# A two-sequence encoder layer with a 16-expert MoE: the last expert's rows added by matrix products instead of a scatter, and the last normalisation moved ahead of the overflow branch

## The chip, the cores and the metric

The kernel runs on one core of one Trainium2 chip. The metric is the device time of one execution in microseconds (us). Engines by the profile's names: PE (TensorE, the matrix unit) with PEld (its weight loads), DVE (VectorE), ACT (ScalarE), POOL (GpSimd) and SP (SyncE, which here only issues DMAs). Each engine runs its own list of instructions in order; they meet only through semaphores.

## The reference, cut to what matters

Two sequences of 256 tokens (T = 512 rows of D = 1024 floats, four tiles of 128 rows) pass a token mixer and then a grouped top-2 mixture of experts:

```python
x = layer_norm(ALPHA * x + token_mixer(x), ln1_g, ln1_b)
# grouped_moe: gates has two nonzero entries in each row of 16
for e in range(16):
    h = silu(xt @ w_e1[e]) * (xt @ w_e3[e])      # 1024 -> 512
    y = y + gates[:, e:e + 1] * (h @ w_e2[e])    # 512 -> 1024
out = layer_norm(ALPHA * x + y, ln2_g, ln2_b)
```

## The kernel before, in words

Weights come as 512 KB units (`load`, L530, on SP's queue) into rings of slots. ACT casts a unit to its float32r high part (`cast_hi`, L680), DVE forms the low part (`cast_lo`, L969), and PE makes three products for each (`three`, L1687 to L1689). In the token mixer the raw ring has six slots and the split ring three, so that the cast of unit u waits until PE has finished unit u - 3. Units 0 to 27 are the input projection; units 0 to 7 and 16 to 27 take 128 columns of the weight (pieces of 512 bytes in DRAM), units 8 to 15 take 512 columns (pieces of 2 KB). In SP's list, after unit 14 and before unit 17, only loads stand; at unit 17 SP stores the value rows (`v_scratch`, L563, 4 x 256 KB), waits for them, and at units 18 and 19 reads them back as windows (`v_win`, L571, 8 x 256 KB, an access pattern whose outer dimension is 4). ACT's list after the cast of unit 19 goes on with `keys(0)` (L711), then the cast of unit 20; PE's list has `scores(0)` (L1723), which needs `keys(0)`, between units 18 and 19.

In the MoE each expert has 128 slots. For each expert a one-hot tile `onehot` (token x slot) gives, by a product on PE, the token, row and gate of each slot; POOL gathers the tokens' rows (`gather`), PE computes the expert (`hidden`, `turn_h`, `output`: the 128 x 1024 result in PSUM banks 2 and 3), ACT scales it by the gates into `y` (`scale_y`, L892) and POOL scatters it (`scatter`, L1621) to `y_dram`, 2T rows: each token has a row in the lower half for its first expert and one in the upper half for its second. `lower_stored` says that experts 0 to 14 are stored; expert 15, the highest, is always a token's second expert, so it never writes the lower half. SP then loads `y_first` (L628, four tiles of 512 KB). After expert 15's scatter `all_stored` rises and SP loads `y_second` (L650).

Should any expert have more than 128 tokens, an `If` on the register loaded from `overflow` (each engine has one) runs further passes over all experts; with these inputs it is not taken and the engines jump to `Else`. In the kernel before this branch stands, on every engine, after expert 15 and ahead of the last sum.

The tail, from L1527 on DVE: for the four tiles x = ALPHA x + y_first (L1529); then for each tile x + y_second (L1535), its statistics (`bn_stats` twice L1538, `bn_aggr` L1540, `var_eps` L1542); POOL takes the root (`root`, L1570 and L1573). Tiles 0 and 1 are scaled on ACT (L954), multiplied by `ln2_g` on POOL (L1668) and get `ln2_b` on DVE (L1548); tiles 2 and 3 are centred and multiplied by `ln2_g` (L1545), then scaled with `ln2_b` (L1552) on DVE. SP stores tile t once it is ready, in the order 0 to 3 (L654), and waits for the stores.

```python
        sp.wait_ge(all_stored, 1)
        for t in range(TT):
            sp.dma_start(y_second[:, t, :], y_dram[T + t * P:T + (t + 1) * P, :]).then_inc(second_loaded[t], 16)
        for t in range(TT):
            sp.wait_ge(out_ready, t + 1)
            ...
        sp.wait_ge(out_stored, 16 * TT)
```

Of the kernel before, what the change touches and what calls it, by code (L numbers as in the profile page):

```python
# [17 lines left out]
P = 128  # L18
# [138 lines left out]
def encoder_layer(nc, A, out_prompt, out_sample):  # L157
# [18 lines left out]

    raw = sb(ctx, "raw", [RAW, UNIT])
# [45 lines left out]
    conv_odd = sb(early, "conv_odd", [W])  # L223
    early.close()
# [40 lines left out]
    y_second = sb(tail, "y_second", [TT, D])  # L265
# [35 lines left out]
    w_lo_more = sb(moe, "w_lo_more", [M_SPLIT - SPLIT, UNIT], F32R)  # L301
    xg = sb(moe, "xg", [2, D])
# [5 lines left out]
    hT_lo = sb(moe, "hT_lo", [4, SLOTS], F32R)  # L308
    y = sb(moe, "y", [2, D])
# [22 lines left out]
    halo_zero = sem("halo_zero")  # L332
    var_ready = sem("var_ready")
# [178 lines left out]
    def _(sp):  # L512
        def load(j, source, n, per=0, i=None):
# [5 lines left out]
            elif j >= U_MOE + RING:  # L519
                sp.wait_ge(lo_cast, nth(j - RING + 1, per, i))  # L520
            elif j == U_MOE:
                sp.wait_ge(unit_used, U_WO)
            elif j == U_MOE + 2 * MORE:
                sp.wait_ge(unit_used, U_WO + 4)
            elif j == U_MOE + 3 * MORE:

                for t in range(TT):
                    sp.wait_ge(x1_ready[t], 1)
                    sp.dma_start(x1_dram[tokens_of(t), :], x1[:, t, :]).then_inc(x1_stored, 16)
# [21 lines left out]
        for u in range(U_MERGE):  # L551
# [5 lines left out]
            if 6 <= u < 14:  # L557
                for qr in range(ROWS):
                    load_bias((u - 6) % 2, (u - 6) // 2, qr)
            if u == 17:  # L560
# [65 lines left out]
        def load_first():  # L626
            for t in range(TT):
                sp.dma_start(y_first[:, t, :], y_dram[tokens_of(t), :]).then_inc(first_loaded[t], 16)  # L628


        sp.wait_ge(flag_ready, 1)
        with sp.register("over_sp") as reg:
            sp.reg_load(reg, overflow[0:1, 0:1])
            with sp.If(sp.snap(reg) > 0):
                with sp.Fori(0, EXPERTS) as e:
# [6 lines left out]
                load_first()  # L642
            with sp.Else():

                sp.wait_ge(lower_stored, 1)
                load_first()

        sp.wait_ge(all_stored, 1)
        for t in range(TT):
            sp.dma_start(y_second[:, t, :], y_dram[T + t * P:T + (t + 1) * P, :]).then_inc(second_loaded[t], 16)  # L650
        for t in range(TT):
            sp.wait_ge(out_ready, t + 1)
            o = (out_prompt, out_sample)[t // 2][0]
            sp.dma_start(o[tokens_of(t % 2), :], x1[:, t, :]).then_inc(out_stored, 16)  # L654
        sp.wait_ge(out_stored, 16 * TT)
# [3 lines left out]
    def _(act):  # L659
# [259 lines left out]
        for k in range(8):  # L919
# [4 lines left out]
            if k == 5:  # L924
                scale_y(j + 5, 15, 1, 0)
            if k == 7:
                scale_y(j + 7, 15, 1, 1)

        act.wait_ge(flag_ready, 1)
        with act.register("over_act") as reg:  # L930
            act.reg_load(reg, overflow[0:1, 0:1])
            with act.If(act.snap(reg) > 0):
                with act.Fori(0, EXPERTS) as e:
# [13 lines left out]
                act.nop()  # L947
            with act.Else():
                act.nop()


        for t in range(TT - 2):
            act.wait_ge(rstd_ready, 10 + t)
            act.activation(x1[:, t, :], x1[:, t, :], ACT.Identity, scale=rstd[:, t:t + 1],  # L954
                           bias=mu_rstd[:, t:t + 1]).then_inc(normalised, 1)
# [3 lines left out]
    def _(dve):  # L959
# [540 lines left out]

        with dve.register("over_dve") as reg:
            dve.reg_load(reg, overflow[0:1, 0:1])
            with dve.If(dve.snap(reg) > 0):
                with dve.Fori(0, EXPERTS) as e:
# [15 lines left out]
                dve.nop()  # L1520
            with dve.Else():
                dve.nop()

        for t in range(TT):  # L1527
            dve.wait_ge(first_loaded[t], 16)
            dve.scalar_tensor_tensor(out=x1[:, t, :], in0=x1[:, t, :], scalar=ALPHA, in1=y_first[:, t, :],  # L1529
                                     op0=ALU.mult, op1=ALU.add).then_inc(final_step, 1)  # L1530
        for t in range(TT):
            row = x1[:, t, :]
            dve.wait_ge(second_loaded[t], 16)
            dve.wait_ge(final_step, max(t + 1, 3 * t + TT))
            dve.tensor_tensor(row, row, y_second[:, t, :], ALU.add).then_inc(y_summed, 1)  # L1535
            dve.wait_ge(y_summed, t + 1)
            for k in range(2):
                dve.bn_stats(stats[:, t, k, :], row[:, k * 512:(k + 1) * 512]).then_inc(final_step, 1)  # L1538
            dve.wait_ge(final_step, TT + 3 * t + 2)
            dve.bn_aggr(mv[:, t, :], stats[:, t, :, :].rearrange("p k s -> p (k s)")).then_inc(final_step, 1)  # L1540
            dve.wait_ge(final_step, TT + 3 * t + 3)
            dve.tensor_scalar(var_eps[:, t:t + 1], mv[:, t, 1:2], EPS, None, ALU.add).then_inc(var_ready, 1)  # L1542
            if t >= 2:
                dve.wait_ge(ln2_loaded, 32)
                dve.scalar_tensor_tensor(out=row, in0=row, scalar=mv[:, t, 0:1], in1=ln2_g[:], op0=ALU.subtract,  # L1545
                                         op1=ALU.mult).then_inc(last_centred, 1)
                dve.wait_ge(scaled, TT + t - 1)
                dve.tensor_tensor(x1[:, t - 2, :], x1[:, t - 2, :], ln2_b[:], ALU.add).then_inc(out_ready, 1)  # L1548
        for t in (TT - 2, TT - 1):
            dve.wait_ge(last_centred, t - TT + 3)  # L1550
            dve.wait_ge(rstd_ready, 10 + t)
# [527 lines left out]
```

## Time and profile before

| | us |
|---|---|
| median of 3 runs (lowest, highest) | 815.1 (814.48, 816.12) |
| the profiled execution: its own time | 817.13 |
| its span on the core, first to last instruction | 815.3 |
| PE busy / DVE / ACT / POOL | 755.7 / 629.7 / 423.8 / 78.6 |
| mean granted clock of PE | 0.958 |

The rows further down come from this one execution; its own time is 1.8 us above its span. The clock is given as a share of 2.4 GHz. Times of rows are us from the span's start. A row of a timeline has start, duration, engine, line, operation, output<-inputs with shapes, the count of merged instructions, and in brackets the idle time before it with what ended it.

### The profile page before, as it was taken

Reading aid. Unit: us, or ns where it says so; the run is one execution under the profiler, and the core shown is the slowest. Engines: PE = TensorE matmul, PEld = TensorE weight load, DVE = VectorE, ACT = ScalarE, POOL = GpSimd, SP = SyncE. Lnnn points to the kernel's source line nnn. Section 1 sums busy time; section 2 is a strip of 40 time slices with the busy share of each in tenths; the row PEclk is TensorE's granted clock in tenths of the full one; section 3 lists DMA queues with packets and bytes.
Section 4 is the critical chain, followed back from the end, with each engine's and each line's share of the span. In section 5 each row is a group of like instructions: output and inputs, shape, how many; then the busy total and the mean of one; then the engine's idle time right before and its main releaser. Section 6 shows DMA issues by size and latency. Waiting matters only on the chain.

```text
span 815.3 us, 10978 instructions
## 1 busy us (share of the span) xinstructions
PE 755.7 (93%) x3559; PEld 621.5 (76%) x3559; DVE 629.7 (77%) x907; ACT 423.8 (52%) x568; POOL 78.6 (10%) x87
## 2 busy tenths in 40 slices
PE   4999999999999999999999859999999999999840
PEld 3888778888888888888888848888888888888630
DVE  5699977766678648344478659999999999999848
ACT  5421235456422246223222418888888888888701
POOL 5000000000000000000110310111111111111006
PEclk9999999999999999999999659999999999999965
DMA  9735556212223332323597548999999999996242
GB/s 300 234 94 145 150 148 164 78 53 77 78 78 104 103 100 79 107 81 101 184 374 246 214 154 279 375 361 368 372 379 377 383 379 373 364 378 236 87 174 104
DMA packets 129167, 171.96 MB, mean 211 GB/s; under 512 B 15386, under 2 KB 67334, under 8 KB 129110
## 3 DMA queue, kind: packets, MB, share of 16 engines
q1 hardware_dynamic: 121440, 154.95, 56.2%
q0 software_dynamic: 6752, 15.80, 5.4%
q10 hardware_dynamic: 934, 0.69, 0.3%
q8 instruction: 23, 0.38, 0.2%
q14 instruction: 18, 0.15, 0.0%
HBM read 164.06 MB, written 15.97 MB: 221 GB/s over the span
## 4 chain that ended last, share of the span: by engine, by line
PE 86%; DVE 7%; ACT 2%; DMA 2%; issue 1%; POOL 1%; DVEq 0%; SPq 0%; POOLq 0%; ACTq 0%
PE bank L1687 26%; PE bank L1689 26%; PE bank L1688 26%; PE bank L1951 2%; PE bank L1723 1%; DMA x_in<-in_x_sample_dram 1%; PE bank L1966 1%; PE bank L1906 1%; PE bank L1733 1%; PE bank L1941 1%; DVE stats L1538 1%; PE bank L1682 1%; ACT w_hi L680 1%; DVE w_lo L969 1%; DVE stats L1271 1%
## 5 line engine op out<-in xcount | busy, mean ns | idle before, releaser
L969 DVE TENSOR_TENSOR w_lo<-raw,w_hi 128x1024 fp32r<-128x1024 f32 x103 | 125.2, 1222 | 80.4 <-ACT w_hi L680 80.1
L680 ACT CAST w_hi<-raw 128x1024 fp32r<-128x1024 f32 x103 | 107.1, 1049 | 105.9 <-PE bank L1689 100.8
L1687 PE MATMUL bank<-xT_hi,w_hi 128*128 128x512 f32 x352 | 140.3, 399 | 2.8 <-DVE xT_lo L1007 1.8
L1689 PE MATMUL bank<-xT_hi,w_lo 128*128 128x512 f32 x352 | 138.7, 394 | 0.0
L1688 PE MATMUL bank<-xT_lo,w_hi 128*128 128x512 f32 x352 | 137.8, 392 | 0.0
L1687 PE MATMUL bank<-w_hi,xgT_hi 128*128 128x512 f32 x192 | 79.4, 413 | 1.6 <-DVE xgT_lo L1434 1.6
L1687 PEld LDWEIGHTS bank<-xT_hi,w_hi 128*128 128x128 f32 x352 | 66.6, 189 | 18.1 <-issue 3.6
L1689 PEld LDWEIGHTS bank<-xT_hi,w_lo 128*128 128x128 f32 x352 | 66.4, 189 | 15.2
L1688 PEld LDWEIGHTS bank<-xT_lo,w_hi 128*128 128x128 f32 x352 | 66.5, 189 | 14.1
L1689 PE MATMUL bank<-w_hi,xgT_lo 128*128 128x512 f32 x192 | 76.2, 397 | 0.0
L1688 PE MATMUL bank<-w_lo,xgT_hi 128*128 128x512 f32 x192 | 75.5, 393 | 0.0
L791 ACT ACTIVATE gate<-bank,vec 128x512 f32<-128x512 f32 x24 | 16.5, 689 | 84.6 <-PE bank L1689 84.5
L969 DVE TENSOR_TENSOR w_lo<-raw_more,w_hi 128x1024 fp32r<-128x1024 f32 x40 | 48.3, 1221 | 8.5 <-ACT w_hi L680 7.8
L969 DVE TENSOR_TENSOR w_lo<-raw_late,w_hi 128x1024 fp32r<-128x1024 f32 x40 | 48.2, 1221 | 3.4 <-ACT w_hi L680 2.7
L680 ACT CAST w_hi<-raw_more 128x1024 fp32r<-128x1024 f32 x40 | 41.2, 1047 | 7.5 <-PE bank L1689 7.5
L1039 DVE SCALAR_TENSOR_TENSOR conv<-conv_in,conv_col,conv 128x512 f32<-128x512 f32 x60 | 44.7, 745 | 0.0
L1689 PEld LDWEIGHTS bank<-w_hi,xgT_lo 128*128 128x128 f32 x192 | 36.5, 190 | 8.7
L1687 PEld LDWEIGHTS bank<-w_hi,xgT_hi 128*128 128x128 f32 x192 | 36.7, 191 | 8.5 <-issue 2.0
L1611 POOL DMA_INDIRECT xg<-x_scratch,slot_token x16 | 20.5, 1278 | 229.4 <-DVE slot_token L1415 119.6
L680 ACT CAST w_hi<-raw_late 128x1024 fp32r<-128x1024 f32 x40 | 41.1, 1048 | 2.7 <-PE bank L1689 2.7
L1688 PEld LDWEIGHTS bank<-w_lo,xgT_hi 128*128 128x128 f32 x192 | 36.8, 192 | 7.0
L1039 DVE SCALAR_TENSOR_TENSOR conv_odd<-conv_in,conv_col,conv_odd 128x512 f32<-128x512 f32 x56 | 41.7, 745 | 0.0
(261 smaller groups left out, 1576.4 us busy)
## 6 DMA issues: line engine op xcount, KB each, us to landing
raw_more<-in_w_e_dram SPq DMA_DIRECT2D x48, 512.0 KB, 7.7
raw<-in_w_e_dram SPq DMA_DIRECT2D x48, 512.0 KB, 7.4
raw_late<-in_w_e_dram SPq DMA_DIRECT2D x48, 512.0 KB, 6.8
raw_rows<-in_w_e_dram SPq DMA_DIRECT2D x48, 512.0 KB, 7.8
raw<-in_w_in_dram SPq DMA_DIRECT2D x28, 512.0 KB, 6.5
raw<-in_w_gate_dram SPq DMA_DIRECT2D x24, 512.0 KB, 3.7
raw<-in_w_o_dram SPq DMA_DIRECT2D x8, 512.0 KB, 3.8
x_scratch<-x_in SPq DMA_DIRECT2D x4, 512.0 KB, 9.4
```

The costliest lines, as they stand in the source:

```text
L680: act.copy(hi_slot(j), raw_slot(j)).then_inc(hi_cast, 1)
L791: act.activation(gate[:, n if n < 2 else r % 2, d, :], bank(name)[:], ACT.Sigmoid, bias=column(V_GATE + n * DC + 2 * r + d)).then_inc(free ...
L969: dve.tensor_tensor(lo_slot(j), raw_slot(j), hi_slot(j).bitcast(F32), ALU.subtract).then_inc(lo_cast, 1)
L1039: o = dve.scalar_tensor_tensor(out=sum_, in0=shifted, scalar=conv_col[:, k, c:c + 1], in1=sum_, op0=ALU.mult, op1=ALU.add)
L1271: dve.bn_stats(stats[:, t, n, :], half).then_inc(dve_step, 1)
L1538: dve.bn_stats(stats[:, t, k, :], row[:, k * 512:(k + 1) * 512]).then_inc(final_step, 1)
L1611: pool.indirect_dma_start(out=xg[:, q, :], out_offset=None, in_=x1_dram, in_offset=bass.IndirectOffsetOnAxis(ap=slot_token[:, q:q + 1], ax ...
L1682: o = pe.transpose(bank(name)[:, k * P:(k + 1) * P], tile(k), ident)
L1687: pe.matmul(out, hi_l, hi_r, start=start, stop=False)
L1688: pe.matmul(out, hi_l, lo_r, start=False, stop=False)
L1689: return pe.matmul(out, lo_l, hi_r, start=False, stop=stop)
L1951: o = pe.transpose(psum[M_XT + half][:, k * P:(k + 1) * P], xg[:, q, c * P:(c + 1) * P], ident)
```

## The change

- **Expert 15 by products.** Its rows are not scattered. ACT and DVE scale its PSUM result by the gates and split it into `y_last_hi` and `y_last_lo`. PE turns the four one-hot tiles (four transposes into bank 7 between `turn_h(15)` and `output(15)`), and ACT copies them back. For each tile of tokens and each half of 512 columns, PE then forms in PSUM: identity times x (plain float32), plus one-hot times `y_last_hi`, plus one-hot times `y_last_lo` (float32r). Here x already holds ALPHA x + y_first + y_second.
- **Zeros.** Since expert 15's rows in `y_dram` stay unwritten, all of `y_dram` (4 MB) is zeroed: eight DMAs of 512 KB from one 128 x 128 tile of zeros, read eight times over, on SP's queue between units 14 and 15.
- **y loads.** `y_first` and `y_second` are loaded tile by tile, alternating, as soon as `lower_stored` is up; `y_second` lies on slots of the raw ring.
- **Statistics from PSUM.** `bn_stats` and the centring (in halves of 512) read the PSUM banks; all four tiles are centred and multiplied by `ln2_g` on DVE. Tiles 0 and 1 are scaled on ACT and get `ln2_b` on POOL; tiles 2 and 3 are finished on DVE as before.
- **Order.** The whole tail, the stores and SP's wait for them stand ahead of the `If`. In the branch taken on overflow, x is reloaded and the tail is done again.

```diff
@@ SP
+            if u == 15:
+                sp.wait_ge(zeros_ready, 1)
+                for t in range(2 * TT):
+                    sp.dma_start(y_dram[tokens_of(t), :].rearrange("p (k n) -> p k n", n=P),
+                                 zeros[:].unsqueeze(1).to_broadcast([P, DC, P])).then_inc(y_zeroed, 16)
...
+        def load_rows():
             for t in range(TT):
                 sp.dma_start(y_first[:, t, :], y_dram[tokens_of(t), :]).then_inc(first_loaded[t], 16)
+                sp.dma_start(y_second[:, t, :], y_dram[T + t * P:T + (t + 1) * P, :]).then_inc(
+                    second_loaded[t], 16)
+        def store_out(again):
+            for t in range(TT):
+                if t < 2:
+                    sp.wait_ge(out_ready, 2 * again + t + 1)
+                else:
+                    sp.wait_ge(last_ready, 2 * again + t - 1)
+                o = (out_prompt, out_sample)[t // 2][0]
+                sp.dma_start(o[tokens_of(t % 2), :], x1[:, t, :]).then_inc(out_stored, 16)
+            sp.wait_ge(out_stored, 16 * TT * (again + 1))
+        sp.wait_ge(lower_stored, 1)
+        load_rows()
+        store_out(0)
         sp.wait_ge(flag_ready, 1)
         with sp.register("over_sp") as reg:
...
@@ ACT, expert 15
             if k == 3:
                 split_hT(15)
+                act.wait_ge(last_turned, 1)
+                act.copy(onehot[:, 1].rearrange("p t s -> p (t s)"), psum[M_INFO][:]).then_inc(last_placed, 1)
+            if k in (5, 7):
+                half = (k - 5) // 2
+                act.wait_ge(unit_used, j + k + 1)
+                act.activation(y_last_hi[:, half * 512:(half + 1) * 512], psum[M_Y + half][:], ACT.Copy,
+                               scale=slot_gate[:, 1:2]).then_inc(last_hi, 1)
+        def scale_last(again):
+            for t in range(2):
+                act.wait_ge(last_centred, 2 * TT * again + 2 * t + 2)
+                act.wait_ge(rstd_ready, 10 + TT * again + t)
+                act.activation(x1[:, t, :], x1[:, t, :], ACT.Copy, scale=rstd[:, t:t + 1]).then_inc(last_scaled, 1)
...
@@ DVE, after expert 15 and ahead of its branch
+        def split_last(half):
+            dve.wait_ge(last_hi, half + 1)
+            dve.scalar_tensor_tensor(out=y_last_lo[:, cols], in0=psum[M_Y + half][:], scalar=slot_gate[:, 1:2],
+                                     in1=y_last_hi[:, cols].bitcast(F32), op0=ALU.mult,
+                                     op1=ALU.subtract).then_inc(psum_free[M_Y + half], 1)
...
+            for k in range(2):
+                dve.wait_ge(final_full, 2 * TT * again + 2 * t + k + 1)
+                dve.bn_stats(stats[:, t, k, :], psum[2 * t + k][:]).then_inc(final_step, 1)
...
+        def centre_last(t):
+            for k in range(2):
+                cols = slice(k * 512, (k + 1) * 512)
+                dve.scalar_tensor_tensor(out=x1[:, t, cols], in0=psum[2 * t + k][:], scalar=mv[:, t, 0:1],
+                                         in1=ln2_g[:, cols], op0=ALU.subtract, op1=ALU.mult).then_inc(
+                    last_centred, 1)
+        def finish(again):
+            last_stats(again, 0)
+            last_stats(again, 1)
+            dve.wait_ge(ln2_loaded, 32)
+            centre_last(0)
+            last_stats(again, 2)
+            centre_last(1)
+            last_stats(again, 3)
+            centre_last(2)
+            centre_last(3)
+            for t in (2, 3):
...
+                dve.scalar_tensor_tensor(out=x1[:, t, :], in0=x1[:, t, :], scalar=rstd[:, t:t + 1], in1=ln2_b[:],
+                                         op0=ALU.mult, op1=ALU.add).then_inc(last_ready, 1)
+        add_rows(0, 0)
+        add_rows(0, 1)
+        split_last(0)
+        add_rows(0, 2)
+        split_last(1)
+        add_rows(0, 3)
+        finish(0)
...
@@ POOL
-        scatter(15, 1)
+            def add_bias(t):
+                pool.wait_ge(last_scaled, 2 * again + t + 1)
+                pool.tensor_tensor(x1[:, t, :], x1[:, t, :], ln2_b[:], ALU.add).then_inc(out_ready, 1)
+            root(2 + again, 0)
+            root(2 + again, 1)
+            add_bias(0)
+            root(2 + again, 2)
+            root(2 + again, 3)
+            add_bias(1)
...
@@ PE
         turn_h(15)
+        for t in range(TT):
+            o = pe.transpose(psum[M_INFO][:, t * P:(t + 1) * P], onehot[:, 1, t, :].bitcast(F32), ident)
+        o.then_inc(last_turned, 1)
         for k in range(4):
             output(15, j + 4 + k, k)
+        def sum_rest(again, t, n):
+            pe.wait_ge(y_summed, TT * again + t + 1)
+            for half in range(2):
+                b, cols = 2 * t + half, slice(half * 512, (half + 1) * 512)
+                pe.wait_ge(*m_drained(b, n - 1))
+                pe.matmul(psum[b][:], ident, x1[:, t, cols], start=True, stop=False)
+        def place_last(t):
+            for half in range(2):
+                b, cols = 2 * t + half, slice(half * 512, (half + 1) * 512)
+                pe.wait_ge(*m_drained(M_Y + half, EXPERTS - 1))
+                pe.matmul(psum[b][:], onehot[:, 1, t, :], y_last_hi[:, cols], start=False, stop=False)
+                pe.matmul(psum[b][:], onehot[:, 1, t, :], y_last_lo[:, cols], start=False, stop=True).then_inc(
+                    final_full, 1)
```

`add_rows(0, t)` on DVE is the ALPHA x + y_first of L1529 followed by the + y_second of L1535 for tile t, and then raises `y_summed`. `form_sum` on PE runs `sum_rest` and `place_last` for tiles 0 to 3 in turn.

## Rows read from the trace of the kernel before

**Rows 1.** The waits of DVE after expert 15 (engine, line, releaser: us in total, times, longest).

```profile
DVE x L1535 <- DMA y_second<-y_scratch: 8.0, 1, 8.0
```

**Rows 2.** Timeline of DVE, 755 to 816 us.

```profile
773.82 0.69 DVE L1444 TENSOR_TENSOR hT_lo<-bank,hT_hi 128x512 fp32r<-128x512 f32 x1 [1.43 <-ACT hT_hi L886]
...
774.76 1.23 DVE L969 TENSOR_TENSOR w_lo_more<-raw_rows,w_hi_more 128x1024 fp32r<-128x1024 f32 x1
779.01 4.63 DVE L1529 SCALAR_TENSOR_TENSOR x<-x,y_first 128x1024 f32<-128x1024 f32 x4 [3.02 <-issue]
...
792.90 1.29 DVE L1538 BATCH_NORM_STATS2 stats<-x 128x6 f32<-128x512 f32 x2
...
794.54 1.22 DVE L1535 TENSOR_TENSOR x<-x,y_second 128x1024 f32<-128x1024 f32 x1
...
800.34 2.49 DVE L1545 SCALAR_TENSOR_TENSOR x<-x,mv,ln_g 128x1024 f32<-128x1024 f32 x1
...
809.60 2.48 DVE L1552 SCALAR_TENSOR_TENSOR x<-x,rstd,ln_b 128x1024 f32<-128x1024 f32 x2
```

**Rows 3.** Timeline of ACT, 755 to 816 us.

```profile
783.18 0.69 ACT L892 ACTIVATE y<-bank,slot_gate 128x512 f32<-128x512 f32 x1 [2.40 <-PE bank L1689]
796.60 1.24 ACT L954 ACTIVATE x<-x,mu_rstd,rstd 128x1024 f32<-128x1024 f32 x1 [12.74 <-POOL mu_rstd L1573]
```

**Rows 4.** Timeline of POOL, 755 to 816 us.

```profile
794.78 1.42 POOL L1570 TENSOR_TENSOR rstd<-var_eps,minus_half 128x1 f32<-128x1 f32 x1 [8.93 <-DVE var_eps L1542]
...
799.41 2.35 POOL L1668 TENSOR_TENSOR x<-x,ln_g 128x1024 f32<-128x1024 f32 x1
...
803.34 1.81 POOL L1573 TENSOR_SCALAR mu_rstd<-mv,rstd 128x1 f32<-128x1 f32 x1
```

**Rows 5.** SP's DMA issues at the end (start, duration, queue, line, transfer, count).

```profile
770.29 1.77 SPq L628 DMA_DIRECT2D y_first<-y_scratch  x4
```

**Rows 6.** The same view, 809 to 816 us.

```profile
809.70 2.73 SPq L654 DMA_DIRECT2D out_dram<-x  x3
```

**Rows 7.** SP's issues around its branch, 738 to 739 us.

```profile
738.88 0.37 SPq L530 DMA_DIRECT2D raw_rows<-in_w_e_dram  x1
```

**Rows 8.** SP's waits over the whole run, columns as in Rows 1.

```profile
SPq L628 <- POOLq L1647: 30.3, 1, 30.3
...
SPq L2033 <- DMA out_dram<-x: 2.5, 1, 2.5
```

**Rows 9.** One line of PE: operation, count, duration min/median/max, first and last start.

```profile
L1830 PE MATMUL bank<-conv_ln,const x2: 590/590/591, 282.4 to 282.8; 128*128 128x512 f32 x2
```

**Rows 10.** Stretches: busy us of each engine, granted clock, DMA share, GB/s.

```profile
773.00:774.00 1.00, 0.17 (x2) 0.00 (x0) 0.18 (x1) 0.80 (x2) 0.00 (x0) 0.87 1.02 414
780.00:781.00 1.00, 1.00 (x5) 0.82 (x4) 1.00 (x2) 0.69 (x1) 0.00 (x0) 0.72 0.00 0
786.00:788.00 2.00, 0.00 (x0) 0.00 (x0) 0.00 (x0) 0.00 (x0) 0.00 (x0) 0.85 0.45 178
```

**Rows 11.** The same view in the input projection.

```profile
78.00:80.00 2.00, 2.00 (x11) 1.58 (x10) 2.00 (x4) 0.00 (x0) 0.00 (x0) 1.00 1.05 400
86.00:88.00 2.00, 2.00 (x10) 1.60 (x9) 2.00 (x4) 0.78 (x1) 0.00 (x0) 1.00 0.00 0
124.00:126.00 2.00, 2.00 (x10) 1.63 (x10) 1.97 (x4) 0.09 (x1) 0.00 (x0) 1.00 1.01 293
```

**Rows 12.** Timeline of ACT, 110 to 145 us.

```profile
121.38 1.05 ACT L680 CAST w_hi<-raw 128x1024 fp32r<-128x1024 f32 x1 [4.28 <-DMA raw<-in_w_in_dram]
122.33 0.69 ACT L711 ACTIVATE kT<-bank,vec 128x512 f32<-128x512 f32 x1
```

**Rows 13.** Timeline of PE, 127 to 137 us.

```profile
127.14 1.58 PE L1723 MATMUL bank<-kT,qT 64*64 64x128 f32 x16
```

**Rows 14.** SP's DMA issues, 0 to 300 us.

```profile
75.51 1.96 SPq L530 DMA_DIRECT2D raw<-in_w_in_dram  x4
...
92.53 3.18 SPq L571 DMA_DIRECT2D v_win<-v_scratch  x4
```

## What the change does to the time, predicted before it ran

> **What bounds the kernel now.** I read the share of busy time first: PE is busy 93% of the span, at full clock nearly throughout, so whatever delays PE ahead of its last product delays the end by as much. The chain of waits then shows that PE's part ends where ACT scales the last half, at 783.18 [rows 3]; 32.1 us of tail follow. In the waits the reader is to see one large one in that tail: DVE stands 8.0 us for y_second [rows 1], whose load must follow expert 15's scatter. From there DVE is busy to 812.08 [rows 2], while POOL turns between it [rows 4]. Last, the stores: three are issued within 2.73 us from 809.70 [rows 6], SP waits 2.5 us for their landing [rows 8], so the first of the three is 5.2 us ahead of the last byte, and 0.3 us later the span ends. The tail is thus DVE's work plus a round trip through DRAM; the head of the change, the zeros, falls into a stage that PE bounds.
>
> **The tail, step by step.** Gone are the scatter, all of the 8.0 us wait, DVE's ln2_b on tiles 0 and 1 and its branch ahead of the sum. The y loads start at 770.29 as before [rows 5]. They are now 4 MB; at the 414 GB/s that they had [rows 10], tile 0 is there by about 775 and tile 3 by 783, each ahead of its use below, so they cost nothing; if they came at half that rate, tile 2 would be late by about 4 us.
>
> ACT's copy of the turned one-hot (0.6 us by a PSUM read of that size, [rows 2], L1444) delays its last cast; DVE's last cast ends at 775.99 + 0.7 = 776.7. PE's four transposes lie in the gap in which it waits for hT_lo at 774.5 [rows 2], and cost nothing; without the gap they would cost 0.6. Then DVE, on its own count:
> - Four times add_rows: 1.24 + 1.26 = 2.5 each [rows 2], 10.0.
> - Two split_last of 128x512 from PSUM: 0.69 each [rows 2], 1.4. The second needs ACT's 783.18 + 0.69 = 783.9 [rows 3]; DVE is there at 784.9 only. This brings DVE to 788.1.
> - Four last_stats: 792.90 to 794.54, 1.64 each [rows 2], 6.6.
> - Four centrings of two halves: 1.3 each (0.69 less the overlap), 5.2. Sum: 799.9.
>
> PE must keep up. A plain float32 product of 512 columns stands as two records of 590 ns that overlap, 1.0 us in all, 0.85 to the next [rows 9]; with four float32r products of 0.23 (one pass each, a quarter of the 0.85 and a little) a tile costs 2 x 0.85 + 4 x 0.23 = 2.6. Tile 0's second half waits for split_last at 785.6; tile 3 is full at about 786.2 + 3 x 2.6 = 794.0, DVE wants it at 795.9. At 1.2 GHz a tile costs 5.2 and tile 3 comes at 804: DVE would stand about 8. The clock was back at 2.4 GHz from 780.6 [rows 10] and PE has no gap over 0.4 us from then on, so I take the full clock.
>
> POOL: a root takes 1.95 us after var_eps, and roots 0 and 1 are early. add_bias(0) needs ACT's scaling (1.24, [rows 3]), runs 794.0 to 796.4 (2.35, [rows 4]); roots 2 and 3 follow. DVE finishes tile 2 at 799.9 to 801.2. L1573 took 1.81 us at 803.34 while DVE ran two-input operations, and L1545 2.49 at 800.34 under POOL's L1668 [rows 2, 4]: one holds the other up for a whole instruction. So root 3 ends with DVE's tile 2, at 801.4, and add_bias(1) and DVE's tile 3 (2.35 + 1.24) follow one after the other, to 805.1. SP stores tile 1 first, so the three stores start between 803.9 and 805.1, and end 5.2 later: 809.1 to 810.3, I take 809.8. The centrings read one operand in PSUM; no row shows such an operation beside POOL's. If they too are held up, 2.1 us are added; if not, none. I take none. The Trainium skill (SBUF — State Buffer, "SBUF: two separate sides") says that the lock concerns DVE operations with two SBUF inputs against a POOL operation that reads SBUF; by it these would be free, and no run here shows it yet.
>
> **The branch at the end.** SP's branch now stands behind its wait for the stores, with nothing left to hide it. Two rows bound it: DVE's own gap at the branch is 3.02 us [rows 2]; SP's last load ended at 739.25 [rows 7] and its next wait began at 770.29 - 30.3 = 739.99 [rows 5, 8], 0.74 us. I take SP's own, 0.7. All other engines' branches end before the stores do. The Trainium skill speaks against this change here (Runtime: NRT & Kernel Launch, "Instruction fetch mechanics"): a taken branch whose target lies outside the window fetched ahead costs a fetch. By that rule it would be nearer DVE's price. Tail: 809.8 + 0.3 + 0.7 = 810.8, against 815.3, a gain of 4.5 (2.2 with DVE's price for the branch).
>
> **The zeros.** Here the sum is uncertain. The queue has a hole: the data of units 13 to 16 (issued from 75.51, [rows 14]) flow at 400 GB/s at 78 to 80 and nothing flows at 86 to 88 [rows 11]; it is empty from about 83 to 88.4, when the v_scratch stores come. 4.19 MB take 10.5 us at 400 GB/s and 14.3 at the 293 that loads with pieces of 512 bytes reach [rows 11]. Then the last unit, v_scratch and v_win (issued at 92.53, [rows 14]) come late by 4.3 to 7.8 us (zeros' time, with units 15 and 16 and the stores queued behind, against 92.4). What waits behind: v_win runs at a quarter of the DMA engines for 20 us, unit 19 queues behind it, and its cast at 121.38 already waited 4.28 us for that load [rows 12]. Behind this cast on ACT stands keys(0), done at 123.02 [rows 12], and PE's scores(0), at 127.14, needs it [rows 13]. So the slack is 4.1 us, and all beyond it stops PE. At 400 GB/s PE waits 0.2 us; at 293, 3.7 us, and a stop of that length brings the clock down: PE stopped at 783.2 and the clock fell within 786 to 788 [rows 10], and the fall at 773 lasted into 780 [rows 10]: from the two means 773.9 to 780.6, and 6.7 us at half the clock give up 3.3. Both ends: 0.2 and 7.0. The stores differ from those loads in that the DRAM side is whole rows of 4 KB and only the SBUF side is in pieces of 512 bytes; so I take the middle rate, 340 GB/s: 12.3 us, late by 5.7, PE waits 1.6, clock kept. The Trainium skill (DMA: Bandwidth & Descriptors, "Specifications") puts the least size for full rate at 512 bytes; by that the zeros would cost nothing, but the 293 against 400 in the rows speaks against it. Everything else added ahead of expert 15 (a memset of 128 columns on POOL, waits long satisfied) is hidden by PE.
>
> **Sum.** 815.3 - 4.5 + 1.6 = 812.4 of span. The profiled execution took 817.13, 1.8 above its span and 2.0 above the median of 815.1; the change of -2.9 put on the median gives 812.2.
>
> **Rivals.**
> 1. *The zeros stop PE and the clock falls.* Place: scores(0) behind keys(0) behind the cast of unit 19. It decides from a lateness of about 7 us on, at a rate of 310 GB/s and less. Time at 293: 815.1 - 4.5 + 7.0 = 817.6; at 220 GB/s (19 us) the stop is 8.5, time 822. For it: the 293, and that the load was late already. Against it: the shape of the DRAM side. Chance 0.33, all but a little of it slower.
> 2. *The zeros are free.* 815.1 - 4.5 + 0.2 = 810.8. For it: the hole of 5 us in the queue. Chance 0.2.
> 3. *The branch costs SP what it costs DVE*, with the forecast's zeros: 812.2 + 2.3 = 814.5. For it: 3.02 is measured, and SP's list behind the If is longer now. Against: SP's own 0.74. Chance 0.12.
> 4. *PE falls to 1.2 GHz in the tail* and DVE stands for tile 3: about 812.2 + 8 = 820. Against: no gap ahead of it. Chance 0.05.
>
> **How the numbers follow.** The forecast, zeros nearly hidden and the tail shorter by 4.5, has 0.30. A measurement here tells 0.2%, 1.6 us. Forecast and rival 2 are faster (0.5, less a little for tails 1 us worse), rival 3 falls within 0.2%, rivals 1 and 4 are slower but for the part of rival 1 at 300 to 310 GB/s. That gives faster 0.48, same 0.17, slower 0.35. The range reaches from rival 2 to rival 1 with the branch at DVE's price: 809.5 to 819.5. The forecast's own range is 811 to 814.
>
> **What will show it.** Zeros: the landing of unit 19 (before 121.3), the start of scores(0) (before 127.1) and the granted clock in the 15 us after it. Tail: DVE without a wait over 0.5 us from 776.7 to 799.9; PE's tile 3 full by 794; add_bias(1) ended by 805; last store landed by 810; the end of the span 1 us behind that, or 3. The forecast is wrong if scores(0) starts later than 129.5, if the clock stands at 1.2 GHz after 785, or if DVE waits on final_full.

## The result, and the profile after

The changed kernel takes 817.91 us (median of 16 runs, 816.42 to 820.52), the kernel before 815.79 us beside it (16 runs, 814.48 to 817.36): ratio 1.0033, 95% interval [1.0024, 1.0042]. It is slower by 0.33%, a side to which I had given a chance of 0.35; the time is 5.7 us above the forecast. The profiled execution took 818.0 us with a span of 816.2, against 817.13 and 815.3.

**Where the time went.** The start of DVE's hT_lo of expert 15 moves from 773.82 [rows 2] to 782.44, so 8.6 us are lost ahead of the tail; from there to the end it is 33.8 us instead of 41.5, so 7.7 us are gained in it. The difference is the 0.9 us between the two spans. Both numbers are larger than forecast, the loss by far.

**The loss.** SP's DMA issues of the changed kernel (start, duration, queue, line, transfer, count), against [rows 14]:

```profile
75.00 0.94 SPq L551 DMA_DIRECT2D raw<-in_w_in_dram  x2
75.98 13.22 SPq L584 DMA_DIRECT2D y_scratch<-zeros  x8
89.25 2.90 SPq L551 DMA_DIRECT2D raw<-in_w_in_dram  x2
92.20 2.83 SPq L589 DMA_DIRECT2D v_scratch<-vs  x4
...
100.20 3.05 SPq L597 DMA_DIRECT2D v_win<-v_scratch  x4
```

The eight zero stores hold SP's queue for 13.22 us. Units 15 and 16 are issued behind them, from 89.25 on (by 77.5 before), and v_win from 100.20 instead of 92.53. Stretches of the same kernel (us of PE, PEld, DVE, ACT, POOL busy, granted clock, DMA share, GB/s), against [rows 11]:

```profile
78.00:80.00 2.00, 2.00 (x10) 1.62 (x9) 2.00 (x5) 0.00 (x0) 0.00 (x0) 1.00 1.01 347
84.00:86.00 2.00, 2.00 (x11) 1.58 (x10) 2.00 (x4) 0.04 (x1) 0.00 (x0) 1.00 1.13 339
...
108.00:112.00 4.00, 1.37 (x5) 0.93 (x4) 4.00 (x8) 1.17 (x1) 0.00 (x0) 0.83 0.38 115
112.00:116.00 4.00, 4.00 (x15) 3.18 (x14) 0.55 (x1) 2.78 (x6) 0.00 (x0) 0.74 0.27 96
...
138.00:142.00 4.00, 1.30 (x15) 1.05 (x14) 2.31 (x5) 2.27 (x6) 0.00 (x0) 0.92 0.36 93
142.00:146.00 4.00, 4.00 (x15) 3.33 (x15) 2.20 (x7) 2.68 (x10) 1.04 (x1) 0.65 0.45 131
```

While the zeros flow, the DMA engines are full at 339 to 348 GB/s. PE then stands three times, and behind the two longer stops the clock goes from 2.4 to 1.2 GHz: cut finer, the granted clock is 0.50 from 111 to 114 and again from 142 to 144. Which waits these are, PE's waits say (engine, line, releaser: us, times, longest). In order of time they are a PSUM bank that DVE empties into `vs`, the keys `kT`, and the softmax's probabilities `probs`; the kernel before had only 0.9 us of the vs wait and neither of the others:

```profile
PE bank L1770 <- DVE probs L1119: 2.7, 1, 2.7
PE bank L1775 <- DVE vs L1174: 2.6, 1, 2.6
PE bank L1811 <- ACT kT L746: 1.2, 1, 1.2
```

Added over 108 to 158 us, PE is busy 43.4 us where it was 49.1 before: 5.6 us more of standing. The granted clock of these 50 us is 0.93, which is up to 3.5 us given up, part of it while PE stood anyway. Together they turn the 1.3 us by which this execution was ahead at 70 us into 7.3 us behind at 163 (ACT's casts), 8.6 in all. ACT's timeline shows the late load itself, with the wait for it in brackets, against [rows 12]:

```profile
96.05 1.05 ACT L715 CAST w_hi<-raw 128x1024 fp32r<-128x1024 f32 x1 [9.04 <-DMA raw<-in_w_in_dram]
...
128.57 1.05 ACT L715 CAST w_hi<-raw 128x1024 fp32r<-128x1024 f32 x1 [9.58 <-DMA raw<-in_w_in_dram]
129.52 0.68 ACT L746 ACTIVATE kT<-bank,vec 128x512 f32<-128x512 f32 x1
```

The first of these casts is of unit 15, the second of unit 19. The longest of the three stops comes at PE's transposes of the probabilities. DVE and PE on the way there, first in the kernel before:

```profile
128.75 0.69 DVE L1062 SCALAR_TENSOR_TENSOR probs<-bank,bias 128x512 f32<-128x512 f32 x1 [0.39 <-PE bank L1723]
...
134.38 0.69 DVE L1076 TENSOR_TENSOR probs<-probs,exp_inv 128x512 f32<-128x512 f32 x1
```
```profile
135.86 0.66 PE L1682 MATMUL bank<-const,probs 128*128 128x128 f32 x4
```

and in the changed kernel:

```profile
141.07 0.69 DVE L1119 TENSOR_TENSOR probs<-probs,exp_inv 128x512 f32<-128x512 f32 x1
```
```profile
141.81 1.11 PE L1770 MATMUL bank<-const,probs 128*128 128x128 f32 x4 [2.70 <-DVE probs L1119]
```

DVE's list between unit 19's cast and the first softmax holds the low parts of units 19 and 20 and four bias adds. In the kernel before DVE stood 0.39 us for PE ahead of that softmax, and its result was there 0.8 us ahead of PE's transposes. So the path from unit 19 over DVE has only 1.2 us of slack.

**The gain.** DVE's timeline in the tail, against [rows 2]; subtract 8.6 to compare:

```profile
782.44 0.69 DVE L1487 TENSOR_TENSOR hT_lo<-bank,hT_hi 128x512 fp32r<-128x512 f32 x1 [1.43 <-ACT hT_hi L921]
...
783.87 1.23 DVE L1012 TENSOR_TENSOR w_lo_more<-raw_rows,w_hi_more 128x1024 fp32r<-128x1024 f32 x1 [0.62 <-ACT w_hi_more L715]
785.01 1.22 DVE L1555 SCALAR_TENSOR_TENSOR x<-x,y_first 128x1024 f32<-128x1024 f32 x1
...
796.19 1.29 DVE L1566 BATCH_NORM_STATS2 stats<-bank 128x6 f32<-128x512 f32 x2
...
805.36 2.72 DVE L1576 SCALAR_TENSOR_TENSOR x<-bank,mv,ln_g 128x512 f32<-128x512 f32 x4
807.99 3.03 DVE L1594 SCALAR_TENSOR_TENSOR x<-x,rstd,ln_b 128x1024 f32<-128x1024 f32 x2
```

DVE waits for nothing from 783.87 to its end at 811.0: the 8.0 us of [rows 1] are gone. POOL beside it, against [rows 4]:

```profile
798.07 0.57 POOL L1648 TENSOR_TENSOR rstd<-var_eps,minus_half 128x1 f32<-128x1 f32 x1 [21.48 <-DVE var_eps L1570]
...
802.12 2.35 POOL L1731 TENSOR_TENSOR x<-x,ln_b 128x1024 f32<-128x1024 f32 x1 [1.59 <-ACT x L973]
...
806.17 0.26 POOL L1651 TENSOR_SCALAR mu_rstd<-mv,rstd 128x1 f32<-128x1 f32 x1
806.39 2.35 POOL L1731 TENSOR_TENSOR x<-x,ln_b 128x1024 f32<-128x1024 f32 x1
```

The two operations of a root take 0.55 to 0.57 and 0.26 us, where POOL in the kernel before took 1.42 to 1.53 for the first and 0.27 to 1.81 for the second. The second add of the bias (2.35 us) ran beside DVE's last centrings; the four took 2.72 us together, 0.68 each, as without company. Its last 0.75 us lay beside DVE's final operation, whose inputs are both in SBUF, and the two of these took 3.03 us instead of the 2.48 of [rows 2].

### The profile page after: what moved, and what is told of

Read it like the earlier page. It is cut to its first block, busy times and chain, and to the rows that moved or that the text cites. A ratio compares the mean times of both kernels' runs of the same rounds, so it can differ in the third digit from the quotient of the medians.

```text
span 816.2 us, 11066 instructions
## 1 busy us (share of the span) xinstructions
PE 769.4 (94%) x3595; PEld 630.7 (77%) x3595; DVE 629.6 (77%) x913; ACT 423.8 (52%) x569; POOL 71.7 (9%) x87
## 4 chain that ended last, share of the span: by engine, by line
PE 82%; DVE 7%; DMA 3%; ACT 2%; SPq 2%; issue 1%; DVEq 0%; POOL 0%; POOLq 0%; ACTq 0%
PE bank L1775 25%; PE bank L1777 24%; PE bank L1776 24%; PE bank L2039 2%; DMA raw<-in_w_in_dram 2%; SPq L597 2%; PE bank L1994 1%; DVE w_lo L1012 1%; PE bank L1770 1%; PE bank L1811 1%; PE bank L2054 1%; PE bank L1821 1%; ACT w_hi L715 1%; DMA v_scratch<-vs 1%; PE bank L2029 1%
```

## The experiments

All ratios are to the kernel before, run on the same chip beside each experiment: 815.92 us beside e1 to e4, 815.68 beside e5 to e8 and 815.87 beside e9 to e11.

**e1: the zeros later, nothing else** (the tile of zeros also lies at another place in SBUF).

```diff
-            if u == 15:
-                ... (SP: eight stores of zeros)
+        pool.wait_ge(unit_used, U_MERGE + 6)
+        for t in range(0, 2 * TT):
+            pool.dma_start(y_dram[tokens_of(t), :]..., zeros...)   # the same eight, by POOL
```

> The changed kernel with its eight DMAs of zeros issued by POOL in the merge stage, after unit 34, in place of SP's list between units 14 and 15; nothing else differs. Theory Z (the zeros, standing in SP's queue ahead of units 15 to 19 and the value rows, stop PE in the input projection; the tail itself is 6 to 8 us shorter): the shift of 8.5 us that the trace shows between 75 and 165 us goes, no cast waits for a weight load that it did not wait for before, and the time is 808 to 810, about 0.992 of the kernel before. Rival T (the tail gains little, and the shift in the head is chance in the clock): the time stays within 2 us of 815.8.

Measured: 808.73 us (808.42 to 809.12), ratio 0.9918 [0.9898, 0.9937]. ACT's timeline:

```profile
121.01 1.05 ACT L713 CAST w_hi<-raw 128x1024 fp32r<-128x1024 f32 x1 [4.47 <-DMA raw<-in_w_in_dram]
```

The cast of unit 19 is where it was in [rows 12]; PE is busy 49.1 us of 108 to 158 again, at full clock. The tail is 33.7 us from hT_lo. So the tail is worth 7.2 us in the medians, and the place of the zeros costs 9.2 (817.91 against 808.73).

**e2: the zeros alone, in the kernel before.**

```diff
             if u == 15:
+                sp.wait_ge(zeros_ready, 1)
+                for t in range(2 * TT): sp.dma_start(y_dram[tokens_of(t), :]..., zeros...)
```

> The kernel before with the same eight DMAs of zeros, the tile, the memset and the waits for them added at the same place, and its tail as it was. Theory Z: 8 to 9 us slower than the kernel before, 824 to 825, ratio 1.010 to 1.011, with the same three stops of PE as in the changed kernel. Rival T: within 2 us of the kernel before.

Measured: 825.96 us (823.82 to 830.11), ratio 1.0132 [1.0104, 1.0159], +10.0 us: a little more than expected. The vs wait is 3.9 us, kT 2.0, probs 1.1. With e1 the two halves stand each by itself, and their sum (-7.2 + 10.0) is near the +2.1 of the whole.

**e3: half of the zeros, at the same place** (the upper half; the lower half of y_scratch isn't cleared).

```diff
-                for t in range(2 * TT):
+                for t in range(TT, 2 * TT):
```

> The changed kernel with only the upper half of y_dram zeroed (four DMAs, 2 MB) at the same place: the lower half is always written by the scatters. At the 345 GB/s that the zeros reached, 2 MB take 6.1 us, against a hole in the queue of 5.6 us, so units 15 to 19 come 0.5 to 1.5 us late and the slack of 4.1 us covers it. Theory Z with a threshold: 808 to 811. If the lost time were proportional to the bytes, half of 8.5 us would stay and the time would be 812 to 813.

Measured: 811.47 us (809.31 to 813.80), ratio 0.9957 [0.9936, 0.9978], 2.7 above e1. The profiled execution is the shortest of the eight, 0.6 above e1's median. SP issues and ACT's cast:

```profile
76.07 6.69 SPq L584 DMA_DIRECT2D y_scratch<-zeros  x4
...
93.70 2.82 SPq L597 DMA_DIRECT2D v_win<-v_scratch  x4
```
```profile
122.78 1.05 ACT L715 CAST w_hi<-raw 128x1024 fp32r<-128x1024 f32 x1 [6.98 <-DMA raw<-in_w_in_dram]
```

Half the zeros make v_win late by 1.2 us, all of them by 7.7: the hole in the queue hides some 5.5 us. PE did not wait for kT at all, as a slack of 4.1 us says; but it waited 1.4 for probs, a second place that my sum did not have. The time lies between the two expectations (up to 811 with a threshold, 812 to 813 in proportion to the bytes), and the interval covers both, so the median does not decide. The trace shows that 5.5 us of the zeros are hidden; what the longer executions lost beyond it was not profiled.

**e4: the zeros on POOL's queue, at 87 us.**

```diff
-            if u == 15:  ... (SP's eight stores)
+        pool.wait_ge(unit_used, 12)
+        for t in range(2 * TT): pool.dma_start(y_dram..., zeros...)
```

> The changed kernel with the eight DMAs of zeros issued by POOL on its own queue, at about the same moment (after unit 11 is used), 512-byte pieces as before. Theory Q (what costs is the order in SP's one queue: loads stand behind the zeros, and SP can't issue them): units 15 and 16 and the value rows share the DMA engines with the zeros instead of waiting for all of them, PE's stops shrink to less than half, 808 to 813. Rival B (what costs is the bandwidth, whatever the queue): as slow as the changed kernel, 816 to 819.

Measured: 822.51 us, ratio 1.0089 [1.0068, 1.011]; the vs wait is 7.5 us. A flawed experiment: the stores were issued at 87.11, 11 us later than in the change and on top of the v_scratch stores, so it changed two things. It tells only that of the moments tried this is the worst. e6 puts that right.

**e5: SP's zeros two units later.**

```diff
-            if u == 15:
+            if u == 17:
```

> The changed kernel with its eight DMAs of zeros on SP's queue two units later: behind units 15 and 16, ahead of the value rows' stores. Theory C (three stops in a chain: the late cast of unit 15 holds DVE, whose work behind it then holds PE at unit 16's banks and drops the clock; the late unit 19 holds keys(0) and the probabilities): the casts of units 15 and 16 are on time, so the first stop (1.7 us and about 1.7 us of half clock) goes; the value rows and unit 19 are as late as before, so the second and third stay: 3 to 4 us faster than the changed kernel's 817.9, 813.5 to 815. Rival (only the lateness of unit 19 counts): no change, 817 to 819.

Measured: 817.11 us, ratio 1.0016 [1.0004, 1.0028]: my theory missed by 2, and the rival, that only the lateness of unit 19 counts, came in. The first stop is gone, the second has grown:

```profile
130.53 1.04 ACT L715 CAST w_hi<-raw 128x1024 fp32r<-128x1024 f32 x1 [11.31 <-DMA raw<-in_w_in_dram]
```
```profile
PE bank L1811 <- ACT kT L746: 5.8, 1, 5.8
```

So the stops are not separate costs: a stop at vs only delays PE on its way to a wait that it would have met anyway. What sets the sum is when unit 19 lands. The traces of all seven kernels with zeros at this place say so, by how much later than in the kernel before two casts of ACT start, that of unit 19 (121.38 there) and that of unit 25 (163.88 there, when all stops are over):

| | unit 19 later by | unit 25 later by | difference |
|---|---|---|---|
| e3 | 1.40 | 0.17 | 1.23 |
| e6 | 6.15 | 4.91 | 1.24 |
| e7 | 6.58 | 5.72 | 0.86 |
| the change | 7.19 | 7.30 | -0.11 |
| e5 | 9.15 | 7.91 | 1.24 |
| e2 | 9.50 | 8.26 | 1.24 |
| e4 | 15.00 | 13.77 | 1.23 |

Five of seven stand 1.2 us below the lateness of unit 19, which is the slack of the path over DVE and the probabilities, however long PE stood for vs or kT before. The change stands 1.3 higher: its last stop was the long one, and the clock at 1.2 GHz from 142 to 144 came behind it with nothing left to absorb it. In e7 PE did not wait for probs: behind the 3.5 us for kT the clock stood below full speed from 128 to 140 us, and PE came to them only after they were ready.

**e6: POOL's queue, at the change's own moment.**

```diff
+        pool.wait_ge(unit_used, 10)          # else as e4
```

> The zeros on POOL's queue as in e4_pool_queue, but issued when unit 9 is used, at 76 us, the moment at which the changed kernel issues them (in e4 they went out at 87 us, on top of the value rows' stores). Theory Q (the order in SP's one queue costs): units 15 and 16 share the engines and land by 88 us, the stores of the value rows at 88 wait only for what is left, 812 to 815. Rival B (the bandwidth costs, by whatever queue): unit 19 as late as in the changed kernel, but units 15 and 16 on time, about as e5; 816 to 818 if they too are late.

Measured: 816.36 us (814.26 to 820.09), ratio 1.0011 [0.9997, 1.0025]; the profiled execution is the shortest of the twelve. POOL's issues, and SP's of the value rows:

```profile
74.78 7.01 POOL L1663 DMA_DIRECT2D y_scratch<-zeros  x8 [57.88 <-PE bank L1777]
```
```profile
87.24 5.74 SPq L584 DMA_DIRECT2D v_scratch<-vs  x4
...
98.54 2.88 SPq L592 DMA_DIRECT2D v_win<-v_scratch  x4
```

SP's loads never stand behind the zeros here, yet v_win is late by 6.0 us and kT's wait is 3.5: another queue gives back 1.6 us of 9.2. So most of the cost is the DMA engines' time and not the order in SP's queue. The casts of units 15 and 16, late in the change, are on time here, and the time is nearly the same.

**e7: the same place, pieces of 2 KB** (a row of 512 zeros read twice, instead of 128 read eight times).

```diff
-  y_dram...rearrange("p (k n) -> p k n", n=P),   zeros...to_broadcast([P, DC, P])
+  y_dram...rearrange("p (k n) -> p k n", n=512), zeros...to_broadcast([P, 2, 512])
```

> The changed kernel with a tile of zeros of 512 columns, so that the pieces are 2 KB in place of 512 bytes; same queue, same place, same bytes. If the size of the pieces costs, the zeros run at 390 to 400 GB/s in place of 345, take 10.6 us in place of 12.2, and everything behind them is 1.5 us less late: 814.5 to 816.5. If it doesn't, 817 to 819.

Measured: 815.57 us, ratio 0.9999 [0.999, 1.0008]. Issues and one stretch:

```profile
76.51 10.05 SPq L587 DMA_DIRECT2D y_scratch<-zeros  x8
```
```profile
82.00:84.00 2.00, 2.00 (x10) 1.62 (x9) 2.00 (x4) 0.00 (x0) 0.00 (x0) 1.00 1.05 406
```

406 GB/s against 343 in the same stretch, and 10.05 us against 13.22: the size of the piece costs 3.2 us of queue and 2.3 us of time. Unit 19's cast comes only 0.6 us earlier than in the change, that of unit 25 1.6; the 1.0 between them goes with the clock, whose last fall came behind the last stop in the change. But with zeros at 406 GB/s the change still gains nothing: kT waits 3.5.

**e8: both remedies**: only the upper half is cleared by stores, in 2 KB pieces, by POOL after unit 34 (the lower half needs none, since each of its rows is written by a scatter).

```diff
+        pool.wait_ge(unit_used, U_MERGE + 6)
+        for t in range(TT, 2 * TT):
+            pool.dma_start(...n=512..., zeros...to_broadcast([P, 2, 512])).then_inc(y_zeroed, 16)
```

> The likely best: the changed kernel with only the upper half of y_dram zeroed, in pieces of 2 KB, by POOL in the merge stage after unit 34. All theories: as e1_late_zeros, 808 to 809.5, since there the zeros cost nothing measurable already.

Measured: 808.55 us (807.79 to 809.42), ratio 0.9907 [0.9892, 0.9923]: the best complete kernel of the study, 9.4 us below the change as it was made, and the same as e1 within what the runs can tell. Its six times stand in two groups, three at 807.8 and three at 809.3 to 809.4.

**e9: e8 without the branch on the overflow flag**, and **e10: the kernel before without it** (both leave out the overflow passes, which these inputs never take). In both the edit is, on every engine:

```diff
-        with sp.register("over_sp") as reg:
-            with sp.If(sp.snap(reg) > 0):
-                ...
```

> The kernel of the late half zeros in 2 KB pieces (808.55 us, span 807.6) without the branch on the overflow flag, on all engines; it leaves out the overflow passes, which these inputs never take. The output stores land about 1.4 us ahead of the end of the span with the branch behind them, and the kernel before had 0.36 us between its last store and the end of the span, so the branch should stand at 1.1 us: about 807.4 us, a ratio near 0.989 to the kernel before. Rival: the branch costs SP what it costs VectorE in the trace of before (3.0 us), 805.5 us. Second rival: nothing, 808.5 us, the time behind the store being the semaphore's own.

> The kernel before without the branch on the overflow flag; it leaves out the overflow passes, which these inputs never take. There VectorE's 3.02 us at the branch lie inside the wait for y_second, which ends with a DMA, so nothing is gained: ratio 1.000, between 0.9990 and 1.0010 (815.0 to 816.5 us). Rival: SP reaches the loads of the tail through its own branch, so the loads of y_second start earlier without it, by 1 to 3 us: 812.8 to 814.8 us.

Measured: e9 806.86 us (806.28 to 807.65), ratio 0.9893 [0.9876, 0.991]; e10 814.96 us against 815.87, ratio 0.999 [0.9979, 1.0]. The medians of e8 and e9 differ by 1.7 us, where I had expected 1.1. From the start of the last three stores to the end of the span it is 7.4 us in e8 (800.16 to 807.6) and 5.6 in e9 (799.44 to 805.0), 1.9 less. This has two parts. From the end of SP's wait for the stores to the end of the span it is 1.4 us in e8 and 0.4 in e9, so 1.0 us is the branch itself, as expected. The other 0.9 lies where I had not looked, in the time from issue to landing of the output stores; the view of that transfer in e8 and in e9:

```profile
DMA to landing us min/median/max: 3.3/3.8/3.8
```
```profile
DMA to landing us min/median/max: 2.6/2.7/2.9
```

That the branch causes the slower landing is not shown: all eight kernels with the new tail and the branch behind it have it (medians of 3.7 to 3.8 us), but e11, which has no branch, has it in part too (2.6 to 4.1, and SP waits 3.6 us for the stores where it waited 2.6 in e9).

In e10 DVE's gap at the branch is gone and turns into wait, span 815.3 as before:

```profile
775.92 4.63 DVE L1465 SCALAR_TENSOR_TENSOR x<-x,y_first 128x1024 f32<-128x1024 f32 x4
791.63 1.23 DVE L1471 TENSOR_TENSOR x<-x,y_second 128x1024 f32<-128x1024 f32 x1 [11.08 <-DMA y_second<-y_scratch]
```

**e11: the centring from SBUF** (e9 with one edit).

```diff
+   act.copy(x1[:, t, cols], psum[2 * t + k][:]).then_inc(sum_copied, 1)     # ACT, behind the statistics
-   dve.scalar_tensor_tensor(out=x1[:, t, cols], in0=psum[2 * t + k][:], ...)
+   dve.scalar_tensor_tensor(out=x1[:, t, cols], in0=x1[:, t, cols], ...)
```

> The kernel of e9 (without the branch, overflow passes left out) with one edit: ScalarE copies the eight half tiles of the sums from PSUM into x1, and VectorE's centring reads x1 in SBUF instead of PSUM, so that both of its tensor operands are in SBUF as are those of GpSimd's adds of the bias and its roots. Theory: an operation of VectorE with two SBUF operands and one of GpSimd hold each other up, so the centring that runs beside GpSimd's 2.35 us add is drawn out and the roots take 1.4 us instead of 0.55 us each; the end comes 2 to 4 us later than in e9. Rival: the reason lies in the order of the tail and not in where the operands are; then only the copies matter, which lie beside VectorE's statistics, and the end moves by less than 0.5 us. In the profile: durations of the eight centrings, of GpSimd's power operations and of its two adds.

Measured: 809.88 us (809.37 to 810.63), ratio 0.9932 [0.9917, 0.9947], 3.0 above e9. POOL in e11:

```profile
789.41 1.00 POOL L1585 TENSOR_TENSOR rstd<-var_eps,minus_half 128x1 f32<-128x1 f32 x1 [0.62 <-DVE var_eps L1534]
...
798.61 3.30 POOL L1673 TENSOR_TENSOR x<-x,ln_b 128x1024 f32<-128x1024 f32 x1
```

and in e9:

```profile
790.30 0.55 POOL L1575 TENSOR_TENSOR rstd<-var_eps,minus_half 128x1 f32<-128x1 f32 x1 [1.28 <-DVE var_eps L1525]
...
797.07 2.34 POOL L1663 TENSOR_TENSOR x<-x,ln_b 128x1024 f32<-128x1024 f32 x1
```

DVE had no gap in e11 and was 0.2 us ahead at 798.4, but the last add started 1.5 us later. About half of this is the edit's own side effect: ACT copies tile 2's sums ahead of scaling tile 0, so that scaling starts at 792.39 instead of 791.57, and with it the first add and root 2 come 0.8 us later. The rest is roots 2 and 3 at 1.0 us instead of 0.55. The last add then ran against DVE's last operation (3.30 us instead of 2.34, and 4.56 for DVE's two tiles, 3.03 in e9). The durations show the theory's sign: with DVE's centrings reading SBUF, POOL's roots are drawn out. Its size they confirm only in part: the profiled spans differ by 2.6 us, of which 1.5 is in the issue of the last store and 1.0 in its slower landing, and of the 1.5 the copies have a share. Of the centrings themselves the last four were drawn out by only 0.6 us (3.33 against 2.71), less than I thought.

## Why the prediction was wrong

**The failed step is "12.3 us, late by 5.7, PE waits 1.6, clock kept".** Its rate of 340 GB/s was right (339 to 348 measured). From there on it failed in three places:
- *The lateness.* The issues took 13.2 us, v_win came 7.7 us later than in [rows 14] and the cast of unit 19 7.2 us later than in [rows 12], not 5.7. In this execution PE was also 1.3 us ahead at 70 us, which widens the gap by as much. I had let the whole hole from 83 to 88 count; e3 against the change puts the hidden part at 5.5 us of 13.2. The 5.7 was also low by its own ends: between 4.3 late for 10.5 us and 7.8 for 14.3, 12.3 us come to 6.0.
- *The path.* I took scores(0) behind keys(0) as the one place where PE can stop, with 4.1 us of slack. That slack was read rightly: PE did not wait there in e3, and in e7 it waited 3.5 with the cast 6.6 late and PE 1.3 ahead (6.6 + 1.3 - 4.1 = 3.8). But the path that binds goes from unit 19 over DVE (the low part, the bias adds, the first softmax) to PE's transposes of the probabilities, and has 1.2 us of slack: behind it PE stood 1.2 us less late than unit 19 in five kernels of seven. A further stop comes earlier, at vs, where DVE's low parts are late because units 15 and 16 are (e5, whose zeros come behind those loads, keeps the 0.9 us of before); it adds nothing to the sum by itself.
- *The clock.* The two stops of over 2 us were each followed by 1.2 GHz. I had this in rival 1, from a lateness of 7 us on. That is where the kernel was, at the middle rate and not at 293 GB/s. Of the two falls only the second shows in the end, with 1.3 us.

So by the casts: 7.2 us late, less 1.2 of slack, plus 1.3 of clock, is the 7.3 us behind at 163, from a start 1.3 us ahead.

Rival 1 is thus nearest to what happened: the zeros stop PE and the clock falls, though the place that binds is the probabilities and not scores(0). It had 7.0 us for the zeros' part; 8.6 stand in the profile and 9.2 between e1 and the change. Its 817.6 is 0.3 from the measured time by luck: the tail made good what the zeros cost more. (Its time with the branch at DVE's price is 817.6 + 2.3 = 819.9, not the 819.5 of the range.) Rival 2 was tested by e7: even at 406 GB/s the zeros are not free. The size of the piece counts, with 2.3 us, but did not decide. The Trainium skill (DMA: Bandwidth & Descriptors, "Specifications") has 512 bytes as enough for the full rate; the trace does not agree, with 343 against 406 GB/s. Rival 4 did not come: the clock was at full rate while PE formed the last tiles, and DVE never waited for it.

**The tail: the mechanism right, 4.5 forecast, 7.7 measured.** By its own marks, times less 8.6: DVE's last cast ends at 776.5 (776.7 forecast), the centrings at 799.5 (799.9), tile 3 is full at 793.9 (794.0), all as said. The mis-sized term is "root 3 ends with DVE's tile 2, at 801.4, and add_bias(1) and DVE's tile 3 follow one after the other": root 3 ended at 797.8 and add_bias(1) ran from 797.8 to 800.1, beside the centring, so the last stores were issued from 800.2 to 802.8 and not from 803.9 on. I had priced roots by rows in which DVE held them up while both of its inputs were in SBUF; beside centrings that read PSUM they take 0.55 us, and 1.0 again in e11. That is 4.3 us better. Against it stand 0.8 us of a slower landing and of the issues, and 0.4 us more at the end than the "0.3 and 0.7".

**The branch.** "I take SP's own, 0.7" was near: 1.0 us by e8 and e9. With it came 0.9 us of slower landing that no term had, which makes 1.9 together; its cause is open. Rival 3 is out at its full price of 3.0. That the branch cost the kernel before next to nothing, since it lay inside the wait for y_second, e10 confirms: that wait grows from 8.0 to 11.1 us, and the median falls by 0.9 us.

**The drift.** Between 163 and 782 us 1.3 us are lost that no wait accounts for. e8, in which PE never stopped for the zeros, loses the same 1.3 us after the same head start, so it is not the zeros' doing; e9 and e11 keep their head start. The casts place the loss between 459 and 492 us (times of the kernel before), in the router, where the granted clock is 0.50 over 460 to 480. From 480 to 500 it is 0.80 in e8 and 0.89 in e9, so it is likely when the clock comes back that differs; why it does stays open.

## What to carry to other kernels

A bulk transfer that "fits a hole in the queue" must be laid against every path that starts from what is queued behind it, through the other engines too, and not only against the one with the known wait. If any of them ends at the bounding engine, put the bulk where the queue is idle for longer than the transfer lasts. Here moving it was worth 9.2 us, more than the 7.2 that the tail gained. And price an operation of GpSimd by a row in which VectorE's neighbour has its operands where yours will have them.

## What the runs showed of the hardware

- Zeros from SBUF to DRAM: 339 to 348 GB/s with source pieces of 512 bytes, 395 to 408 with pieces of 2 KB, though whole rows of 4 KB are written in both (the change over 78 to 86 us, e7 over 80 to 88).
- Issued on another queue, the same zeros still made v_win 6.0 us late, 7.7 on its own queue (e6, the change).
- A centring of VectorE with one operand in PSUM (0.68 us per 128x512) and GpSimd's add (2.35) run side by side without loss; with centrings whose inputs are all in SBUF GpSimd's root grows from 0.55 to 1.0 us, and its add, beside VectorE's last operation, from 2.34 to 3.30 (e9, e11). The Trainium skill (SBUF — State Buffer, "SBUF: two separate sides") says so of VectorE's operations with two SBUF inputs; the trace agrees.
- A stop of PE of 1.4 us left the granted clock at 1.00 (e3, 132 to 140 us); behind one of 2.7 us it stood at 0.65 over 142 to 146 (the change).
- SP's taken branch at the end of the kernel costs 1.0 us (e8, e9).
